# Attention's value products in plain float32 instead of three high and low products

## The reference, cut to what matters

```
s = einsum(q_c, kc) * scale;  p_cmp = masked_softmax(s, valid)      # 31 compressed blocks
o_cmp = einsum(p_cmp, vc)
s = einsum(q_c, kg) * scale;  p = masked_softmax(s, mask_s)         # selected keys
o_slc = einsum(p, vg)
s = einsum(q_c, kwc) * scale; p = masked_softmax(s, mask_w)         # window keys
o_win = einsum(p, vwc)
return g[0] * o_cmp + g[1] * o_slc + g[2] * o_win
```

## Time and profile before

| | |
|---|---|
| median of 3 runs | 1833.69 us (1833.57 to 1836.84) |
| profiled execution | 1839.77 us, its span 1837.9 us |
| TensorE busy | 1793.4 us, 98% of the span |
| VectorE, ScalarE, GpSimd busy | 48%, 33%, 6% |
| granted TensorE clock, mean | 0.993 of full speed |

### The profile page before, as it was taken

How to read it: one execution, slowest core, us unless ns; L and a number is a source line. 1 busy time by engine, 2 the same in 40 slices (tenths; PEclk the granted TensorE clock), 3 DMA queues, 4 the chain that set the end, 5 groups by cost and what they waited for, 6 DMA issues and landing times.

```text
span 1837.9 us, 22546 instructions
## 1 busy us (share of the span) xinstructions
PE 1793.4 (98%) x8308; PEld 1480.0 (81%) x8308; DVE 877.6 (48%) x1135; ACT 615.0 (33%) x894; POOL 105.2 (6%) x93
## 2 busy tenths in 40 slices
PE   8999999999988899999999999999999999999999
PEld 6888888877767777888888888888888878888887
DVE  5544443366777755444443344444432554444322
ACT  5333332234345644333232232333222432333211
POOL 0500000122010001000000000000000110000000
PEclk9999999999998999999999999999999999999999
DMA  5333333324310003333343323333332223333331
GB/s 173 92 103 91 102 110 96 89 82 101 84 57 13 0 19 89 99 92 102 91 122 101 98 80 93 101 91 103 116 100 64 75 81 92 102 91 114 103 102 48
DMA packets 321363, 163.70 MB, mean 89 GB/s; under 512 B 13893, under 2 KB 320041, under 8 KB 321322
## 3 DMA queue, kind: packets, MB, share of 16 engines
q1 hardware_dynamic: 321130, 163.08, 30.8%
q10 hardware_dynamic: 192, 0.08, 0.0%
HBM read 161.04 MB, written 2.10 MB: 89 GB/s over the span
## 4 chain that ended last, share of the span: by engine, by line
PE 90%; DVE 6%; ACT 2%; issue 1%; DMA 0%; SPq 0%; DVEq 0%; POOL 0%; ACTq 0%
PE ps_s L541 19%; PE ps_s L543 19%; PE ps_s L542 19%; PE ps_y L541 9%; PE ps_y L543 9%; PE ps_y L542 9%; DVE w_lo L1411 1%; PE ps_aux L541 1%; DVE pt_b L1801 1%; DVE xg_lo L1429 1%; ACT scratch L1281 1%; PE ps_aux L542 1%; PE ps_aux L543 1%; ACT w_hi L1021 1%; DVE small L1759 0%
## 5 line engine op out<-in xcount | busy, mean ns | idle before, releaser
L1411 DVE TENSOR_TENSOR w_lo<-raw,w_hi 128x1024 fp32r<-128x1024 f32 (+2 forms) x279 | 367.6, 1318 | 735.1 <-ACT w_hi L1021 734.6
L541 PE MATMUL ps_s<-xg_hi,w_hi 128*128 128x512 f32 x1608 | 632.1, 393 | 8.0 <-DVE xg_lo L1429 5.6
L543 PE MATMUL ps_s<-xg_hi,w_lo 128*128 128x512 f32 x1608 | 626.4, 390 | 0.0
L542 PE MATMUL ps_s<-xg_lo,w_hi 128*128 128x512 f32 x1608 | 626.2, 389 | 0.0
L1021 ACT CAST w_hi<-raw 128x1024 fp32r<-128x1024 f32 (+2 forms) x279 | 312.1, 1119 | 596.7 <-PE ps_s L543 302.7
L541 PEld LDWEIGHTS ps_s<-xg_hi,w_hi 128*128 128x128 f32 x1608 | 302.1, 188 | 77.3 <-DVE xg_lo L1429 8.3
L542 PEld LDWEIGHTS ps_s<-xg_lo,w_hi 128*128 128x128 f32 x1608 | 302.2, 188 | 64.2 <-issue 2.4
L543 PEld LDWEIGHTS ps_s<-xg_hi,w_lo 128*128 128x128 f32 x1608 | 302.1, 188 | 63.4
L541 PE MATMUL ps_y<-act_hi,w_hi 128*128 128x512 f32 x704 | 274.3, 390 | 0.7 <-DVE w_lo L1411 0.7
L543 PE MATMUL ps_y<-act_hi,w_lo 128*128 128x512 f32 x704 | 273.9, 389 | 0.0
L542 PE MATMUL ps_y<-act_lo,w_hi 128*128 128x512 f32 x704 | 273.9, 389 | 0.0
(11 more groups left out here) (326 smaller groups left out, 1189.7 us busy)
## 6 DMA issues: line engine op xcount, KB each, us to landing
raw<-in_ffn_w_gate SPq DMA_DIRECT2D x88, 512.0 KB, 3.9
raw<-in_ffn_w_up SPq DMA_DIRECT2D x88, 512.0 KB, 3.9
raw<-in_ffn_w_down SPq DMA_DIRECT2D x64, 704.0 KB, 4.6
raw<-in_hyb_w_in SPq DMA_DIRECT2D x19, 512.0 KB, 3.8
x_in<-in_x SPq DMA_DIRECT2D x8, 256.0 KB, 6.1
raw<-in_hyb_cmp_w SPq DMA_DIRECT2D x4, 512.0 KB, 4.0
raw<-in_hyb_w_in SPq DMA_DIRECT2D x8, 256.0 KB, 3.3
raw<-in_hyb_w_out SPq DMA_DIRECT2D x16, 128.0 KB, 2.9
```

The costliest lines, as they stand in the source:

```text
L541: mm(bank, hi, x_hi, start=first, stop=False, **kw)
L542: mm(bank, hi, x_lo, start=False, stop=False, **kw)
L543: return mm(bank, lo, x_hi, start=False, stop=last, **kw)
L1411: tt(w_lo[:, n % 2, 0:size], raw[:, n % 4, 0:size], f32(w_hi[:, n % 2, 0:size]), ALU.subtract).then_inc(lo_ready, 1)
```

## The change

The values and the turned probabilities are no longer split. ScalarE copies each once, as plain float32 (`v_t`, `vc_t`, `ptc`, and `pt_even` and `pt_odd` for the turned probabilities), VectorE does nothing to them, and TensorE multiplies them with one plain float32 matmul a block. The copies raise the semaphores that the low parts raised: `pt_ready` for `turn` and `values`, `c_pt_ready` for `scores_c` and `values`, `aux_free` in the projections. `values` gets a wait on `o_lo_ready`, so that the output of the pair before has been read. The even pairs' turned probabilities have an area of their own; both areas begin where `pt_b` lay, which is used only in the projections.

```diff
+            with ExitStack() as blocks_ctx:
+                pt_b = sb("pt_b", [P, 2, 4 * T], F32R, blocks_ctx)
+            pt_even = mb("pt_even", [P, 2, 2, 2, P])
+            pt_odd = mb("pt_odd", [P, 2, 4, 2, P])
...
-                at_least(pe, pt_lo_ready, 8 * j + s)
+                at_least(pe, pt_ready, 8 * j + s)
...
-                pe.wait_ge(pt_lo_ready, 8 * j + 2 * pair + 2)
+                pe.wait_ge(pt_ready, 8 * j + 2 * pair + 2)
...
-                pe.wait_ge(c_pt_lo_ready, 2 * j + pair // 2 + 1)
-                three(bank, vc_hi[:, :], vc_lo[:, :], ptc[:, 0, queries], ptc[:, 1, queries], True, False)
+                pe.wait_ge(c_pt_ready, 2 * j + pair // 2 + 1)
+                at_least(pe, o_lo_ready, 4 * j + pair)
+                mm(bank, vc_t[:, :], ptc[:, queries], start=True, stop=False)
                 for br in range(2):
                     for k in range(2 * half_pair + 2):
-                        at = (br * 4 + k) * 2 * P
-                        last_mm = three(bank, v_hi[:, br, k * P:(k + 1) * P], v_lo[:, br, k * P:(k + 1) * P],
-                                        p_hi[:, at:at + 2 * P], p_lo[:, at:at + 2 * P],
-                                        False, br == 1 and k == 2 * half_pair + 1)
+                        last_mm = mm(bank, v_t[:, br, k * P:(k + 1) * P], probs[:, br, k, :, :], start=False,
+                                     stop=br == 1 and k == 2 * half_pair + 1)
...
-                copy(v_hi[:, br, :], ps_aux[:, :]).then_inc(v_hi_ready, 1)
+                copy(v_t[:, br, :], ps_aux[:, :]).then_inc(aux_free, 1)
...
-                copy(vc_hi[:, :], ps_aux[0:NCP, 0:P]).then_inc(v_hi_ready, 1)
+                copy(vc_t[:, :], ps_aux[0:NCP, 0:P]).then_inc(aux_free, 1)
...
-                copy(ptc[:, 0, :], ps_stat[0:NCP, :]).then_inc(c_pt_hi_ready, 1)
+                copy(ptc[:, :], ps_stat[0:NCP, :]).then_inc(c_pt_ready, 1)
...
-                p_hi = turned_parts(pair % 2)[0].rearrange("p (b k h q) -> p b k h q", b=2, k=4, h=2)
-                copy(p_hi[:, :, 0:c + 1, c % 2, :],
-                     ps_y[:, :, 0:(c + 1) * P].rearrange("p b (k q) -> p b k q", q=P)).then_inc(pt_hi_ready, 1)
+                probs = turned(pair % 2)
+                copy(probs[:, :, 0:c + 1, c % 2, :],
+                     ps_y[:, :, 0:(c + 1) * P].rearrange("p b (k q) -> p b k q", q=P)).then_inc(pt_ready, 1)
...
-            def values_low(br):
-                dve.wait_ge(v_hi_ready, br + 1)
-                tt(v_lo[:, br, :], ps_aux[:, :], f32(v_hi[:, br, :]), ALU.subtract).then_inc(aux_free, 1)
...
-                tt(vc_lo[:, :], ps_aux[0:NCP, 0:P], f32(vc_hi[:, :]), ALU.subtract).then_inc(aux_free, 1)
...
-                tt(ptc[:, 1, :], ps_stat[0:NCP, :], f32(ptc[:, 0, :]), ALU.subtract).then_inc(c_pt_lo_ready, 1)
...
-                tt(p_lo, ps_y[:, :, 0:(c + 1) * P].rearrange("p b (k q) -> p b k q", q=P), f32(p_hi),
-                   ALU.subtract).then_inc(pt_lo_ready, 1)
```

More of the change, by code:

```diff
@@ L232, in build @@
             kc_lo = mb("kc_lo", [P, 2, NCP], F32R)
[L233 to L236, removed]
+            v_t = mb("v_t", [P, 2, NQ * P])
+            vc_t = mb("vc_t", [NCP, P])
             ob_hi = mb("ob_hi", [P, 4 * T], F32R)
@@ L239, in build @@
             prob = mb("prob", [P, 2, PW])
-            pt_b = mb("pt_b", [P, 2, 4 * T], F32R)
             prob_c = mb("prob_c", [P, NQ, NCP])
-            ptc = mb("ptc", [NCP, 2, T], F32R)
+            ptc = mb("ptc", [NCP, T])
             m1 = mb("m1", [P, T])
@@ L321, in build @@
         k_lo_ready = sem("k_lo_ready")
-        v_hi_ready = sem("v_hi_ready")
         blk_step = sem("blk_step")
@@ L351, in build @@
         c_pt_done = sem("c_pt_done")
[L352 to L355, removed]
+        c_pt_ready = sem("c_pt_ready")
+        pt_ready = sem("pt_ready")
         pv_done = sem("pv_done")
@@ L389, in head_tiles, with turned @@
             return STATS.index(name) - STATS.index("ks") + 1
[L391 to L395, removed]
+        def turned(slot_):
+            return pt_odd[:, :, :, :, :] if slot_ else pt_even[:, :, :, :, :]
         def prob_of(s):
@@ L825, in scores_c @@
                 if g or not isinstance(j, int):
-                    pe.wait_ge(c_pt_lo_ready, 2 * j + g)
+                    pe.wait_ge(c_pt_ready, 2 * j + g)
                 for c in range(NQ):
@@ L1171, in odd_keys, with take_values @@
                 copy(e[DH:P, :, 0:T - 1], e[0:DH, :, 1:T]).then_inc(odd_ready, 1)
-            def split_values(br):
+            def take_values(br):
                 act.wait_ge(aux_done, AUX.index("t_vs") + br + 1)
-                copy(v_hi[:, br, :], ps_aux[:, :]).then_inc(v_hi_ready, 1)
+                copy(v_t[:, br, :], ps_aux[:, :]).then_inc(aux_free, 1)
             def split_blocks(c):
@@ L1222, in _ @@
             split_blocks(0)
-            split_values(0)
+            take_values(0)
             split(U_W1 + 1)
             split_blocks(1)
-            split_values(1)
+            take_values(1)
             split(U_W1 + 2)
@@ L1293, in exps_c, with take_c, take_probs @@
                 last.then_inc(c_exp_done, 1)
-            def split_c(j, g):
+            def take_c(j, g):
                 act.wait_ge(c_pt_done, 2 * j + g + 1)
-                copy(ptc[:, 0, :], ps_stat[0:NCP, :]).then_inc(c_pt_hi_ready, 1)
-            def split_probs(j, s):
+                copy(ptc[:, :], ps_stat[0:NCP, :]).then_inc(c_pt_ready, 1)
+            def take_probs(j, s):
                 j, s = j + s // 8, s % 8
@@ L1322, in attend @@
                     if not (first and s == 0):
-                        split_probs(j, s - 1)
+                        take_probs(j, s - 1)
                     if not (last and s == 7):
@@ L1326, in attend @@
                     if s in (2, 6):
-                        split_c(j, s // 4)
+                        take_c(j, s // 4)
                     if s in (0, 4) and not (first and s == 0):
@@ L1341, in _ @@
             split_output(3, 2)
-            split_probs(3, 7)
+            take_probs(3, 7)
             split_output(3, 3)
@@ L1629, in _ @@
             scaled(U_MIX + 5, 5, vt[:, :])
-            values_low(0)
             split(U_W1 + 1)
@@ L1633, in _ @@
             scaled(U_MIX + 6, 6, vt[:, :])
-            values_low(1)
             split(U_W1 + 2)
@@ L1747, in kc_low @@
                    f32(kc_hi[:, :, :].rearrange("p a b -> p (a b)")), ALU.subtract).then_inc(kc_ready, 1)
-                dve.wait_ge(v_hi_ready, 3)
-                tt(vc_lo[:, :], ps_aux[0:NCP, 0:P], f32(vc_hi[:, :]), ALU.subtract).then_inc(aux_free, 1)
             def maxima(j, s):
@@ L1818, in attend @@
                         output_low(j, (s - 4) // 2)
[L1819 to L1822, removed]
                     if s in (0, 4) and not (first and s == 0):
@@ L1839, in _ @@
             output_low(3, 2)
-            probs_low(3, 7)
             output_low(3, 3)
@@ L1974, in _ @@
             for slot_ in range(2):
[L1975 to L1978, removed]
+                zeros = turned(slot_)[:, :, 2 * slot_ + 1, 0, :]
+                last = tt(zeros, consts[:, 0:2 * P].rearrange("p (b q) -> p b q", b=2),
+                          consts[:, 0:2 * P].rearrange("p (b q) -> p b q", b=2), ALU.subtract)
             last.then_inc(probs_zeroed, 1)
```

3 lines of the change are left out of this document (removed).

## The result

| | before | changed |
|---|---|---|
| median, run together | 1836.51 us (5 runs, 1833.57 to 1837.41) | 1825.79 us (5 runs, 1824.55 to 1827.87) |
| profiled execution | 1839.77 us, span 1837.9 | 1824.55 us, span 1822.4 |
| granted TensorE clock, mean | 0.993 | 0.998 |

The ratio is 0.994 with a 95% interval of 0.9918 to 0.9962: faster, by some 10.7 us or 0.6%. In later runs beside the experiments the changed kernel had 1826.01 us against 1835.54 (0.9947, interval 0.9934 to 0.9961). The forecast was 1825.3.

A forecast was written before the change was run, and what follows sets the result against it. TensorE, busy for 1793.4 of 1837.9 us, was taken as the bound, so only its waits could yield time. From the median 1833.7, the sum of -6.7 and the clock's -1.7 gave 1825.3 us, range 1822 to 1829.

The forecast's parts named there:

- The walk of one half: Half a head on TensorE in attention, turn of c = 0 to the next: 0.85 us gained from 15.43 us.
- late next: TensorE's new wait before the next scores, for ScalarE's exponentials of c = 3: half a microsecond.
- The block: Each value product block as one plain float32 matmul of two records, 0.215 us each: 7.8 us more in all.
- The six halves: Six halves of heads in attention after the first: 0.85 us gained in each, -5.1 us together.
- The first half: First half in attention: the 1.85 us wait before the turn at 556.23 falls entirely, -1.85 us.
- The last half and the end: End of attention: a 0.93 us wait loses 0.65, three products grow by 0.57, 0.25 and 0.57: +0.75 us.
- The rotation: Projections, at 527.14: its 0.89 us wait for the low part of the compressed values shortens, -0.5 us.
- The added wait: Value products also wait for the low part of the previous pair's output: cost nothing, at most 0.37 and 0.42 us.
- The clock: Three low-clock stretches of TensorE in the attention loop cost 8.4 us; the smallest, 1.7 us, was taken as gone.
- first rival: TensorE's clock stays up all through: -15.1 us, 1818.6 or about 1823.7 us; chance 0.17.
- The second rival: Exponentials are the next chain, blocks cost 0.226 us a record, clock gives nothing: 1829 to 1833 us; chance 0.19.
- The third: Slower: each plain matmul's second weight load is not hidden, 24 us on TensorE, 1851 us; chance 0.09.

The follow-up runs named there:

- the variant with VectorE's copy: The changed kernel with the turned probabilities of c = 1 copied on VectorE instead of ScalarE: 1821.8 us, later 1822.44 against the changed kernel's 1826.01.
- the low parts back in the chain: The changed kernel with VectorE again subtracting after each copy of probabilities, result unused, before TensorE may go on: 1842.26 us, 1.0028 of before.
- the lows beside it: The changed kernel with three fast products a block (compressed stays plain), high and low parts made from ScalarE's copy by GpSimd and VectorE: 1842.0 us, 1.0028 of before.
- the fast products: The changed kernel with each value block as three fast matmuls of the same copies, no low parts: 1816.69 us, 0.9886 of before.
- the doubled blocks: The changed kernel with every plain value product issued twice into the same bank: 1873.99 us, 1.0207 of before.

## Why the prediction was right, and where its sizes were off

**The walk of one half** held nearly to the row. From V, the end of the long product (557.84 now):

| | forecast | measured |
|---|---|---|
| turn c = 2 | V + 1.6 | V + 1.60 |
| scores, behind the exponentials | V + 2.74 | V + 2.72 |
| short product | V + 3.6 | V + 3.61 |
| turn c = 3 | V + 5.95 | V + 6.06 |
| next turn c = 0 | V + 9.02 | V + 8.96 |

The wait named as late next is there, in every one of the six halves, 0.25 to 0.30 us by the record (the hand-over from the turn lies beside it; taking the exponentials out of the way gave half a microsecond).

**The block** was sized right at 0.215 us a record (0.216 measured), and the term that failed is "18 x 0.215 + 0.2": the start of a product is 0.29 us, not 0.2. I had read 0.26 from the fast product and then took less. The long product grew by 0.68, not 0.57, the short one by some 0.35, not 0.25. The Trainium skill ("FP8 and Floating Point Precision", TensorE Precision Notes) has four passes for true float32. Those are 4 x 256 columns at 2.4 GHz, an estimate of 0.427 us a block, and the rows agree with 0.432; but a block of three float32r products took 0.36 as the earlier trace rows have it and not the 0.32 of its columns, so a block cost 0.07 more and not the 0.107 that counting passes gives.

**The six halves** gained 0.52 us each and not 0.85. Of the difference 0.11 is that start, and 0.12 more passes between the turn of c = 0 and the long product (1.61 us for 1.49). It lies between that turn and the scores behind it (0.26 for 0.14 us); for its cause no run was made. The rest is the choice of the half: the earlier trace rows hold one of 15.43 us, while the six of before, 100.10 us less the 8.4 of low clock, average 15.28.

**The first half** gained 1.95 against 1.85, but not as told: before, a second wait stood in it, which the walk overlooked:

```profile
547.71 0.85 PE L849 MATMUL ps_y<-consts,scratch 128*128 128x128 f32 x6 [1.45 <-DVE xg_lo L1801]
```

It is gone in the profile too, since TensorE ran that stretch at the low clock (6.8 us in place of 3.4) and so came later to what it had waited for. In the second profile of the variant with VectorE's copy the low stretch is shorter, and a wait of 1.33 us stands at this place, for VectorE's copy. That copy, from 545.95 to 546.64, stands behind the maxima and the scaling in VectorE's queue, and the first half takes 13.00 us, against 12.98 in the first profile of the same kernel.

**The last half and the end** lost 1.0 against 0.75, again the growth of its products. In detail, the short product there still waits 0.90 us, now for ScalarE's copy of the compressed probabilities:

```profile
647.76 0.85 PE L845 MATMUL ps_y<-consts,scratch 128*128 128x128 f32 x6 [0.33 <-ACT pt_even L1016]
649.51 0.66 PE L858 MATMUL ps_aux<-ptc,vc_t 32*128 32x256 f32 x2 [0.90 <-issue]
```

That copy ends at 649.41, behind the exponentials in ScalarE's queue. With no scores of a next head between, the product comes 0.76 us sooner after the long product than before (V + 3.11 for V + 3.87), so the removed low part did give its part, and the wait that is left is the copy's own.

**The rotation** in the projections waits 0.34 us for 0.89: 0.55 against the 0.5 of the sum.

```profile
525.13 1.12 PE L711 MATMUL ps_aux<-work,consts 128*128 128x512 f32 x2 [0.34 <-ACT vc_t L1016]
```

**The added wait** on `o_lo_ready` cost nothing, as told: no row names it. **The sum** of these is -0.55 - 1.95 - 3.1 + 1.0 = -4.6, where -6.7 stood.

**The clock** was the other term that was off, the other way. I took 1.7 us of a possible 8.4; in the profiled executions all 8.4 came back, and the mean granted clock over attention rose from 0.93 to 0.98. So the first rival's condition held in the profile, and its -15.1 against the profiled execution is what was measured (-15.2), though of that some 2.3 lie outside what the change touches (the late data and the two low stretches named above) and cover what the sum lacks. The medians moved by 10.7 and 9.5 us in the two sets of runs; less the 4.6 this leaves 5 to 6 us. The granted clock of the runs beside the experiments says that most of this is the clock: it averages 0.9943 over the nine of before and 0.9976 over the five of the changed kernel, and times the span that is, as an estimate, 10.4 and 4.4 us of lost time, 6.0 between them, where the mean times differ by 9.7. With the low parts back in the chain it is 0.9945 over eleven runs, the level of before. The reason against that rival, that after the wait at 607.50 the clock did not fall, was true of one wait and said little about a kernel with none. The two errors, 2.1 too much gain in the sum and 3 to 4 too little in the clock, largely cancel, so it is in part luck that the number came out within half a microsecond; the median of before was also 2 to 3 us higher in the later runs than the 1833.7 that the forecast started from.

What decides the clock is not settled, but the nine profiles narrow it. In attention, behind the entry, they hold eleven low stretches. Nine are in the three kernels with waits of 0.8 us and more through the loop (three before, two with the lows back in the chain, four with the lows beside it), and each begins inside such a wait or at most 2.1 us after it. The six profiles of kernels without such waits in the loop hold two, both in the last half: the fast products' from 643.1 to 646.5 us and the doubled blocks' from 694.2 to 697.7, which begin 0.7 and 1.2 us behind the wait of 0.90 us that both have there (at 642.46 and 693.09). The changed kernel has the same wait and its clock stayed up in both profiles. So none of the eleven began away from a wait of 0.8 us or more, yet many such waits are passed at full clock, the 1.18 us at 607.50 among them. Plain blocks do not prevent a fall; whether they make it rarer is open, as the two falls in the last half are one of fast and one of plain products.

The second rival was half right: the exponentials are the next chain, at the 0.3 us it named, and the blocks cost more than forecast, but its "the clock gives nothing" did not hold, as the 6.0 us above show. The third, a weight load that shows, is excluded by the doubled blocks: 0.216 us a record, where it needed 0.245.

## What to carry to other kernels

A conversion that releases a single buffer is priced by its place between two users of that buffer, not by its engine's load: here 29 us of VectorE work weighed by the 28 waits of up to 1.8 us that it stood behind, not by its sum. Moved beside the chain, with its rounding on VectorE and GpSimd, it stood behind another wait and gave nothing. It can pay to make the busiest engine's work a fifth dearer (0.43 for 0.36 us a block) if that takes a step of another engine out of the chain that it waits for. And after such a change look at once for what the freed engine can take over from the one that is now waited for; here that was another 3.6 us for one copy.

## What the runs showed of the hardware

**GpSimd holds up VectorE's scaling.** In the kernel with GpSimd's rounding, the scaling pair of 128x512 on VectorE took some 2.5 us in seven places, each beside GpSimd's operation on 128x768, and 1.00 us in the changed kernel. In the eighth place, at 663.27, GpSimd's operation began only when the pair was almost done, at 664.20, and the pair took its usual time. The one of 596.94 above, beside it on GpSimd, and the pair of the changed kernel:

```profile
597.10 2.08 POOL L1988 TENSOR_TENSOR xg_hi<-pt_odd,consts 128x768 fp32r<-128x768 f32 x1 [3.91 <-ACT pt_odd L1026]
```

```profile
560.65 1.00 DVE L1774 TENSOR_SCALAR scratch<-scratch,small,gate 128x512 f32<-128x512 f32 x2
```

The Trainium skill ("GPSIMD Engine Reference", Specifications) has GpSimd's SBUF interface shared with VectorE, with contention for VectorE's two-port modes and for two SBUF inputs; the rows agree with a contention, though they do not show in which mode the scaling ran. VectorE does not merely slow down: in all seven places the second scaling of the pair ends 0.28 to 0.29 us after GpSimd's operation, whether that took 1.85 or 2.09 us, as if it had stood still until then. It costs VectorE 1.5 us each time.

**Fast products that repeat their operands are cheaper.** With the same values and probabilities three times, the starts of 23 records take the 2.62 us from 569.09 to 571.71, 0.114 each, where high and low parts took 0.120. So that run flatters the fast form by some 0.25 us a half, 42 x 0.006, and the price of the plain blocks is nearer 0.9 us a half than 1.2.

**A low clock can be free.** The two profiles of the copy on VectorE are of one kernel, one with 6.8 us of low clock at the entry and one with 3.4. Their first halves take 12.98 and 13.00 us: at the higher clock TensorE waited 1.33 us there, at the lower one it did not wait.
